# Attention with feature-major outputs: exponentials first, then the transposes of two steps back

## The reference

```python
h = rms_norm(x, g_attn) * (1.0 + scale_a) + shift_a
proj = h @ w_in                       # q_a k_a v_a c_q c_kv k_r
q_a, k_a = rope(rms_norm(q_a)), rope(rms_norm(k_a))
o_a = block_attention(q_a, k_a, v_a)  # group A: 8 query heads, 2 key heads, 64 wide
q_b = rms_norm(c_q, g_cq) @ w_uq      # group B: 8 heads, 64 plain + 32 rotary
kv  = rms_norm(c_kv, g_ckv) @ w_ukv   # keys and values of group B; k_r is shared
o_b = block_attention(q_full, k_full, v_b)
o = concatenate([rms_norm(o_a, g_out_a), rms_norm(o_b, g_out_b)]) @ w_o
x = x + gate_a * o
h = rms_norm(x, g_ffn) * (1.0 + scale_f) + shift_f
u = depthwise_conv_centred(h @ w_up, conv_w, conv_b)
x = x + gate_f * ((silu(gate) * val) @ w_down)
```

## Time and profile before

| | us |
|---|---|
| median of three runs | 1194.02 |
| the profiled execution, whole | 1194.76 |
| its span, first to last instruction | 1193.0 |
| PE busy | 1165.8 (98%) |
| DVE busy | 728.9 (61%) |
| POOL busy | 568.4 (48%) |
| ACT busy | 534.5 (45%) |

### The profile page before, as it was taken

One profiled execution on the slowest core, in us unless ns is written; L12 is line 12 of the kernel. 1 busy time (PEld: TensorE's weight loads), 2 busy tenths in 40 slices (PEclk: granted clock), 3 DMA queues, 4 the chain that ended last, 5 costly groups with the idle time before them and its releaser, 6 DMA issues.

```text
span 1193.0 us, 18770 instructions
## 1 busy us (share of the span) xinstructions
PE 1165.8 (98%) x6288; PEld 997.4 (84%) x6288; DVE 728.9 (61%) x1481; ACT 534.5 (45%) x866; POOL 568.4 (48%) x768
## 2 busy tenths in 40 slices
PE   9999999999999999999999999999999999999997
PEld 6897887998888888888789979889888888888886
DVE  5878986767766677757666438746775134412345
ACT  5347675254431344234354677635543234422432
POOL 2487500655655445644665540054555544454462
PEclk9999997999999999999999999999999999999998
DMA  9743333423445444544433202222343322332322
GB/s 350 307 168 116 92 103 107 141 72 132 174 139 207 133 166 176 194 141 176 141 110 119 75 1 89 89 89 71 124 141 106 106 86 90 106 106 74 102 89 71
DMA packets 43979, 151.55 MB, mean 127 GB/s; under 512 B 5122, under 2 KB 7810, under 8 KB 43908
## 3 DMA queue, kind: packets, MB, share of 16 engines
q1 hardware_dynamic: 43908, 150.64, 36.6%
HBM read 148.52 MB, written 2.10 MB: 126 GB/s over the span
## 4 chain that ended last, share of the span: by engine, by line
PE 46%; issue 24%; POOL 15%; POOLq 6%; DVE 6%; DVEq 2%; ACT 1%; ACTq 0%
POOL w_lo L535 14%; PE ps L614 14%; PE ps L620 14%; PE ps L615 14%; POOLq L536 5%; DVE ada_prod L1387 2%; DVEq L1389 1%; DVE nmx L1758 1%; PE ps L749 1%; PE ps L950 1%; PE ps L738 1%; PE ps L718 0%; DVE ada_prod L1608 0%; DVE o_sb L1771 0%; PE ps L726 0%
## 5 line engine op out<-in xcount | busy, mean ns | idle before, releaser
L535 POOL TENSOR_TENSOR w_lo<-w_raw,w_hi 128x256 fp32r<-128x256 f32 x712 | 532.1, 779 | 599.3 <-ACT w_hi L1117 575.7
L614 PE MATMUL ps<-h_hi,w_hi 128*128 128x512 f32 (+1 forms) x960 | 349.7, 364 | 4.2 <-DVEq L1561 2.2
L615 PE MATMUL ps<-h_lo,w_hi 128*128 128x512 f32 (+1 forms) x960 | 347.3, 362 | 0.0
L620 PE MATMUL ps<-h_hi,w_lo 128*128 128x512 f32 (+1 forms) x960 | 347.2, 362 | 0.0
L1117 ACT CAST w_hi<-w_raw 128x1024 fp32r<-128x1024 f32 x178 | 183.2, 1047 | 183.8 <-PE ps L614 183.6
L614 PEld LDWEIGHTS ps<-h_hi,w_hi 128*128 128x128 f32 x960 | 181.7, 189 | 36.8 <-DVEq L1561 3.8
L1809 DVE SCALAR_TENSOR_TENSOR u_sb<-ps,par,u_sb 128x510 f32<-128x510 f32 x176 | 131.7, 748 | 123.2 <-ACT u_sb L1345 110.2
L620 PEld LDWEIGHTS ps<-h_hi,w_lo 128*128 128x128 f32 x960 | 181.7, 189 | 27.5
L615 PEld LDWEIGHTS ps<-h_lo,w_hi 128*128 128x128 f32 x960 | 181.8, 189 | 27.2
L614 PE MATMUL ps<-a_hi,w_hi 128*128 128x512 f32 (+1 forms) x400 | 146.6, 366 | 3.3 <-DVEq L1595 2.4
L620 PE MATMUL ps<-a_hi,w_lo 128*128 128x512 f32 (+1 forms) x400 | 145.6, 364 | 0.0
(11 more groups left out here) (160 smaller groups left out, 1372.6 us busy)
## 6 DMA issues: line engine op xcount, KB each, us to landing
w_raw<-w_slots SPq DMA_DIRECT2D x178, 512.0 KB, 3.5
ada_raw<-ada_slots SPq DMA_DIRECT2D x88, 512.0 KB, 3.8
shift<-shift_slots SPq DMA_DIRECT2D x8, 512.0 KB, 13.2
x_tok<-x_rows SPq DMA_DIRECT2D x4, 512.0 KB, 9.6
x<-x_t SPq DMA_DIRECT2D x4, 512.0 KB, 13.7
y_t<-x SPq DMA_DIRECT2D x3, 512.0 KB, 2.9
y_t<-x SPq DMA_DIRECT2D x1, 256.0 KB, 3.0
y_t<-x SPq DMA_DIRECT2D x2, 128.0 KB, 2.7
```

Source lines behind the costliest of these rows:

```text
L535: nc.gpsimd.tensor_tensor(w_lo[:, j, c], w_raw[:, j, c], w_hi[:, j, c].bitcast(F32), ALU.subtract)
L614: hh = mm(out, stat[0], mov[0], start=first, stop=False)
L615: hl = mm(out, stat[0], mov[1], start=False, stop=False)
L620: return mm(out, stat[1], mov[0], start=False, stop=last)
```

## The change

- Outputs are made with features on partitions: the values are the stationary operand (64 columns for each of two heads, side by side in the array), the transposed probabilities move, 256 columns. No column of ones: ScalarE's exponentials sum their rows as they go (`accum_out`), and the probabilities are scaled before they are transposed, two of the four row blocks by VectorE, two by GpSimd (`scale_rows`).
- The transposes of the outputs and those of group B's queries go. Group B's queries are computed with features on partitions; the weights for their rotary part carry a second, swapped copy of the columns, and VectorE multiplies with a table of cosines and sines (`q_table`, one load more). Group B's scores are made of two products, plain and rotary.
- The sum of squares over features for the output norms is GpSimd's (`add_squares`) and a product of TensorE with ones (`group_sums`); ScalarE takes roots and VectorE reciprocals over the whole of 512 or 256 columns in PSUM.
- Fills, keys and one of the values are copied by VectorE instead of ScalarE, the outputs too.
- The pipeline is one step deeper. TensorE does in iteration i fill(i+1), scores(i), prob_transposes(i-2), outputs(i-3). ScalarE makes the exponentials of i first, behind a wait for the transposes of i-2, and then copies those transposes.
- The first four tiles of the output projection are each made in two parts: all first parts (group A), then all second parts.

The diff, cut to its core:

```diff
...
+    def scale_rows(j):
+        pool.wait_ge(rin_ready, NP * L + j + 1)
+        for c in (2, 3):
+            nc.gpsimd.tensor_scalar(prob[:, j % 2, c, :], prob[:, j % 2, c, :], rinv[:, j, c:c + 1], None,
+                                    ALU.mult)
+        nc.gpsimd.drain()
+        pool.sem_inc(second_scaled, 1)
+    def add_squares(j):
+        group, s, _ = PAIRS[j]
+        k, c = pair_tile(j), slice(s * SEQ, (s + 1) * SEQ)
+        total = (ssum if group == "a" else ssq_b)[:, c]
+        pool.wait_ge(o_done, NP * L + j + 1)
+        if k % 4 == 0:
+            nc.gpsimd.tensor_tensor(total, o_t[:, k, c], o_t[:, k, c], ALU.mult)
+        else:
+            nc.gpsimd.tensor_tensor(o_sq[:, 0, :], o_t[:, k, c], o_t[:, k, c], ALU.mult)
+            nc.gpsimd.drain()
+            nc.gpsimd.tensor_tensor(total, total, o_sq[:, 0, :], ALU.add)
+        nc.gpsimd.drain()
+        pool.sem_inc(o_summed, 1)
+    for i in range(NP + 1):
+        if i < NP:
+            scale_rows(i)
+        if i >= 2:
+            add_squares(i - 2)
+        if 2 <= i < 14:
+            n = L * SLOTS + S_WO + 1 + (i - 2) // 4
+            lo_quarter(n % RING, n, (i - 2) % 4)
+    lo_slots(L * SLOTS + S_WO + 4, L * SLOTS + SLOTS)
...
+def out_part(L, m, ks, release=0):
     j = slot(L, S_WO + m)
     if 0 in ks:
         wait_free(pe, L, ("wo", m))
+        pe.wait_ge(exp_ready, 4 * (NP * (L + 1) - int(m < 2)))
     for k in ks:
+        last_event = k if k < KD // 2 else k + KD // 2
+        pe.wait_ge(ot_ready, N_EVENTS * L + last_event + 1)
+        last = product(ps[:, bank(("wo", m)), :], [r[:, j, k * P:k * P + P] for r in (w_hi, w_lo)],
+                       out_operand(k, slice(0, T)), k == 0, k == KD - 1, release * int(k == ks[0]))
     if KD - 1 in ks:
+        last.then_inc(full[bank(("wo", m))], 1)
...
         pe.wait_ge(pt_ready, NP * L + j)
         for u in range(2):
+            if u == 1:
+                pe.wait_ge(second_scaled, NP * L + j + 1)
             for q in range(2):
+                if u == 0:
+                    pe.wait_ge(first_scaled, 2 * (NP * L + j) + q + 1)
...
+        for k in range(2):
+            for u in range(2):
+                v = va[:, 2 * s + k, u, :] if group == "a" else vb[:, 2 * s + k, heads[u], :]
+                last = mm(ps[64 * u:64 * u + 64, O_BANK, 0:SEQ], v, prob_t[:, j % 2, u, k, :],
+                          start=(k == 0), stop=(k == 1))
         last.then_inc(o_full, 1)
...
+    def group_sums(n):
+        pe.wait_ge(o_summed, (NP - 1) * L + (NA, NA + 4, NP - 1)[n])
+        if n == 0:
+            pe.wait_ge(qt_ready, NA * (L + 1))
+            total = ssum[:]
+        else:
+            pe.wait_ge(on_ready, N_EVENTS * L + KD // 2)
+            total = ssq_b[:, (n - 1) * SEQ:n * SEQ]
+        last = mm(sum_view(n), ones[:], total, start=True, stop=n < 2)
+        if n == 2:
+            pe.wait_ge(last_sq, L + 1)
+            last = mm(sum_view(n), ones[:], o_sq[:, 1, :], start=False, stop=True)
+        last.then_inc(group_sum, 1)
+    expand_values(0)
+    fill(0)
+    expand_values(1)
+    for i in range(NP + 3):
+        if i + 1 < NA:
             fill(i + 1)
+        if i < NP:
             scores(i)
         if i == 0:
+            expand_values(2)
+            expand_values(3)
+            expand_keys(0)
+        if i == 1:
+            expand_keys(1)
+            expand_keys(2)
+        if i == 2:
+            expand_keys(3)
+        if i == NP + 1:
+            out_part(L, 0, (0, 1))
         if 0 <= i - 2 < NP:
+            prob_transposes(i - 2)
+        if 0 <= i - 3:
+            outputs(i - 3) if i < NP + 2 else None
+        if i == NA + 3:
+            group_sums(0)
+        if i == NP - 1:
+            group_sums(1)
+    out_part(L, 0, (2, 3))
+    outputs(NP - 1)
+    out_part(L, 1, range(KD // 2))
+    group_sums(2)
     for m in range(2, TAIL):
+        out_part(L, m, range(KD // 2))
+    for m in range(TAIL):
+        out_part(L, m, range(KD // 2, KD), int(m > 0))
...
+def group_roots(L, n):
+    act.wait_ge(group_sum, 3 * L + n + 1)
+    A(sum_view(n), sum_view(n), ACT.Sqrt, bias=eps[:], scale=1.0 / 512).then_inc(group_root, 1)
+def output_hi(L, e):
+    k, c, hi, _ = event(e)
+    act.wait_ge(on_ready, N_EVENTS * L + e + 1)
+    nc.scalar.copy(hi, o_t[:, k, c]).then_inc(on_hi_ready, 1)
...
+    def take_transposes(j):
+        act.wait_ge(pt_full, NP * L + j + 1)
+        if j >= 2:
+            act.wait_ge(o_full, NP * L + j - 1)
+        nc.scalar.copy(prob_t[:, j % 2, :, :, :],
+                       ps[:, PT_BANK:PT_BANK + 2, :].rearrange("p u (k q) -> p u k q", k=2)
+                       ).then_inc(pt_ready, 1)
+    take_values(0)
+    take_values(1)
+    for i in range(NP + 2):
         if i == 0:
+            take_values(2)
+        if i >= 2:
+            act.wait_ge(pt_full, NP * L + i - 1)
+        if i < NP:
             act.wait_ge(max_ready, NP * L + i + 1)
             for c in range(4):
                 A(prob[:, i % 2, c, :], ps[:, S_BANK[i % 2] + c // 2, (c % 2) * SEQ:(c % 2 + 1) * SEQ],
+                  ACT.Exp, bias=nmx[:, i, c:c + 1], accum_out=rsum[:, i, c:c + 1]).then_inc(exp_ready, 1)
+        if i >= 2:
+            take_transposes(i - 2)
+        if i == 4:
+            split_hi(L, S_WO + 2)
+        if i == 8:
+            split_hi(L, S_WO + 3)
+        if i == NA + 4:
+            group_roots(L, 0)
+        if NA + 5 <= i < NA + 9:
+            output_hi(L, i - NA - 5)
+        if i == NP:
+            prepare(ACT.Sqrt)
+            group_roots(L, 1)
+    for e in range(KD // 2, KD):
+        output_hi(L, e)
+    group_roots(L, 2)
+    for e in range(KD, N_EVENTS):
+        output_hi(L, e)
...
+def group_inverse(L, n):
+    dve.wait_ge(group_root, 3 * L + n + 1)
+    V.reciprocal(sum_view(n), sum_view(n))
     V.drain()
+def output_scaled(L, e):
+    k, c, _, _ = event(e)
+    V.scalar_tensor_tensor(out=o_t[:, k, c], in0=o_t[:, k, c], scalar=par[:, L, PC_GOUT + k:PC_GOUT + k + 1],
+                           in1=sum_view(e // (KD // 2)), op0=ALU.mult, op1=ALU.mult).then_inc(on_ready, 1)
+def output_lo(L, e):
+    k, c, hi, lo = event(e)
+    dve.wait_ge(on_hi_ready, N_EVENTS * L + e + 1)
+    V.tensor_tensor(lo, o_t[:, k, c], hi.bitcast(F32), ALU.subtract).then_inc(ot_ready, 1)
...
+    for p in range(HEADS // 2):
+        key = ("uq", HEADS // 2 + p)
+        wait_full(dve, L, key)
+        V.tensor_tensor(halves(qr[:, p, :]), halves(ps[:, bank(key), :]),
+                        tq[:].rearrange("p (o t) -> p o t", o=1).broadcast_to([P, NSEQ, SEQ]), ALU.mult)
+        V.drain()
+        dve.sem_inc(free[bank(key)], 1)
     ada_at(L, ("in", 2))
+    def take_fill(j):
+        dve.wait_ge(qt_full, NA * L + j + 1)
+        if j >= 2:
+            dve.wait_ge(s_full, NP * L + j - 1)
+        V.tensor_copy(q_t[:, j % 2, :], ps[:, QT_BANK, 0:SEQ])
+        V.drain()
+        dve.sem_inc(qt_ready, 1)
...
+    def scale_rows(j):
+        dve.wait_ge(exp_ready, 4 * (NP * L + j + 1))
+        V.reciprocal(rinv[:, j, :], rsum[:, j, :])
+        V.drain()
+        dve.sem_inc(rin_ready, 1)
+        for c in range(2):
+            V.tensor_scalar(prob[:, j % 2, c, :], prob[:, j % 2, c, :], rinv[:, j, c:c + 1], None,
+                            ALU.mult).then_inc(first_scaled, 1)
+    def take_outputs(j):
+        _, s, _ = PAIRS[j]
+        k, c = pair_tile(j), slice(s * SEQ, (s + 1) * SEQ)
+        o = ps[:, O_BANK, 0:SEQ]
+        dve.wait_ge(o_full, NP * L + j + 1)
+        V.tensor_copy(o_t[:, k, c], o)
+        V.drain()
+        dve.sem_inc(o_done, 1)
...
+    take_fill(0)
+    for i in range(NP + 1):
+        if i + 1 < NA:
+            take_fill(i + 1)
         if i < NP:
+            maxima(i)
+        if i == 0:
+            take_values(3)
+            take_keys(0)
+        if i == 1:
+            take_keys(1)
+        if i >= 1:
+            scale_rows(i - 1)
+        if i == 1:
+            take_keys(2)
+        if i == 2:
+            take_keys(3)
+        if i < NP:
             ada_step(L, i, 0)
+        if i >= 3:
+            take_outputs(i - 3)
         if i < NP:
             ada_step(L, i, 1)
+        if i == NA + 5:
+            group_inverse(L, 0)
+            output_scaled(L, 0)
+            output_scaled(L, 1)
+        if i == NA + 6:
+            output_lo(L, 0)
+            output_scaled(L, 2)
+        if i == NA + 7:
+            output_lo(L, 1)
+            output_scaled(L, 3)
+        if i == NP:
+            output_lo(L, 2)
+            output_lo(L, 3)
+    take_outputs(NP - 2)
+    group_inverse(L, 1)
+    for e in range(KD // 2, KD):
+        output_scaled(L, e)
+    take_outputs(NP - 1)
+    for e in range(KD // 2, KD):
+        output_lo(L, e)
+    group_inverse(L, 2)
+    for e in range(KD, N_EVENTS):
+        output_scaled(L, e)
+    for e in range(KD, N_EVENTS):
+        output_lo(L, e)
```

More of the change, by code:

```diff
@@ L106, with pair_tile @@
 NP = len(PAIRS)
-VW = HD + 1
+NA = NP // 2
+def pair_tile(j):
```

(42 more changed lines are left out.)

418 lines of the change are left out of this document (138 added, 280 removed).

## The result

The changed kernel takes 1240.66 us (median of 4 runs, 1239.37 to 1242.52) against 1193.44 for the kernel before (4 runs, 1190.72 to 1194.55): a ratio of 1.040, 95% interval 1.0378 to 1.0423. The forecast was 1228 with a range of 1204 to 1248: slower, the side that was forecast, and 12.7 us beyond the number. The profiled execution has a span of 1240.7 us where it was 1193.0, so 47.7 us are to be found.

The account below looks back on a forecast made before the run. It took VectorE to pace the steps with adaLN, TensorE's step being hardly longer in layer 1. 1194.02 + 25.0 (layer 1) + 6.0 (layer 2) + 3 (behind the projection) = 1228 us, range 1204 to 1248.

Parts of the forecast that it names:

- Start of layer 1: Before layer 1's attention: first maximum at 113.6, +8.5 us, as VectorE waits for the last query products before its adaLN.
- Steps of layer 1: Layer 1's 16 attention steps: 108.0 us against 82.5, +25.5, with port, copies and group A's norm included.
- The port: Attention steps: VectorE and GpSimd wait for each other's instructions, 0.8 us a step taken, bounds 0 and 1.5.
- the halves stay at 1.22 beside a busy GpSimd: Steps with adaLN: a sign that the forecast is wrong; it expected adaLN halves of more than 1.22 us.
- The reciprocal of 512 columns: Group A's norm, once a layer on VectorE: 3.1 us, bounds 0.5 to 3.1.
- rival (4): Attention steps: the new order doesn't decouple engines, late GpSimd work holds quick steps; +13 us; chance 0.08 with worse.
- rival (2): Attention steps: TensorE, busy some 60% of a step, gets the lower clock for stretches; about +13 us, 1241; chance 0.20.
- Tail of layer 1: From the steps' end to the output projection's last full tile: 26.8 us against 35.8, -9.0.
- Behind the projection: After the output projection: late slot release and four x updates within 11 us beside adaLN, +3 us for both layers.
- Layer 2: Second layer's attention: start +2.7, steps +7.5 (eight without adaLN at 3.9 us each), tail -4.2; together +6.0 us.
- Rival (1): Attention steps: the port costs nothing, half of GpSimd's work can lie behind PSUM reads; -17 us, 1211; chance 0.18.
- Rival (3): Attention steps: TensorE paces and its savings pass through if VectorE's adaLN step stays under about 4.9; 1188; chance 0.09.

Follow-up runs that it names:

- e4: Group B's first-sequence sum stands on TensorE behind step 14's transposes and step 13's outputs, against the changed kernel: 1235.32 us.
- the kernel with everything together: Changed kernel plus ScalarE copying outputs and group A's fills, tail sum and two adaLN products moved, GpSimd scaling rows by TENSOR_TENSOR: 1224.90 us.

## Why the prediction was right in sign and 13 us short

By its own steps, in the profiled execution:

- **Start of layer 1**: +8.5 forecast, +7.8 measured, by the mechanism named; the run with the adaLN products moved shows that 5 of it was their place.
- **Steps of layer 1**: +25.5 forecast, +22.7 measured (20.6 between the maxima, and a last step of 6.8 instead of 4.7). The list of VectorE's instructions was right: 5.1 forecast in group B without collisions, 5.22 measured. The port was half as dear as taken, 0.41, and fell on other instructions. The prediction named as a sign against it that the halves stay at 1.22 beside a busy GpSimd, and in the repeated step they do: the price is on the pair of row scalings, 1.09 instead of 0.61. The reciprocal of 512 columns took 3.37 (forecast 3.1), and shortening it gave 2.9 a layer. The step of 6.87 wasn't forecast: GpSimd had fallen behind, TensorE waited 2.2 us for it and then made its scores at the lower clock. That is rival (4) with a piece of rival (2), for single steps; with short scalings on GpSimd it is 5.63.
- **Tail of layer 1**: -9.0 forecast. From the last step's end at 218.2 to TensorE's end of the second halves at 249.2 it is 31.0 where it was 35.8, so -4.8. The term that failed is the 26.8 us for the new tail: it left out a wait that the change adds. The sum over group B's first sequence goes into the PSUM bank of group A's, may start only when VectorE's last scaling has read that, and stands on TensorE ahead of the transposes of step 14. With the sum moved the tail is 27.5.
- **Behind the projection**: +3 for both layers forecast, with the reason right (x is updated four times within 11 us beside adaLN) and the size wrong. From TensorE's end (223.5, now 249.2) to ScalarE's first copy of the feed-forward part it was 43.5 us and is 49.7, +6.2 in layer 1 alone; with short adaLN halves it is 43.7. Before and after:

```profile
267.04 1.43 ACT L1345 ACTIVATE u_sb<-ps,par 128x512 f32<-128x512 f32 x2
```

```profile
298.93 1.43 ACT L1374 ACTIVATE u_sb<-ps,par 128x512 f32<-128x512 f32 x2
```

- **Feed-forward of layer 1**: nothing forecast, +0.2 measured.
- **Layer 2**: start +2.7 forecast, +2.6 measured. Steps +7.5 forecast, +12.0 measured (9.9 and a last step of 6.8). The quick ones took 4.2 instead of 3.9. The 3.9 came from GpSimd's list, and GpSimd doesn't hold them: emptied, it leaves them at 29.1. The ring of 4.01 us through TensorE and ScalarE does, which "ScalarE is close by", 3.3 us, left out. It is the first half of rival (4), that the new order doesn't decouple the engines. The odd 5.81 adds the lower clock: outputs of 1.98 us where they take 1.08, and 4.28 in e4, whose granted clock was 1.00 there. The steps with adaLN hold two of the 6.87 kind (6.91 and 7.35, TensorE waiting 1.84 and 2.22 us for GpSimd's scaling). Here the GpSimd row scaling is the mis-sized term, 0.98 us without a collision (1.96 a pair) and 1.3 on average, not 0.45. The nearest row of the kernel before, with half the columns and a constant factor, already took 0.53:

```profile
L553 POOL TENSOR_SCALAR gqk<-gqk 128x128 f32<-128x128 f32 x1 | 0.5, 533 | 0.3 <-issue 0.3
```

The tail and the rest of layer 2: -2.7 forecast, +1.1 measured: the same wait at the sum, 5.98 us there.

The misses add up: -0.7 - 2.8 + 4.2 + 4.7 + 0.2 - 0.1 + 4.5 + 3.8 = 13.8, against 47.7 - 34.0 = 13.7 (1.5 of the 3 is counted in each layer). Two of the errors worked against each other: with the measured 0.41 for the port's 0.8 in 24 steps, the sum would have been 9 us lower, 1219. So the port's price, twice too high, covered part of what was left out, and a miss of only 13 us is in part luck. The measured time is that of rival (2), 1241, but not by its mechanism: at the full clock the repeated steps kept their length. Rival (1) was tried by emptying GpSimd: 9.3 us, not 17. Rival (3) fell with VectorE's back-to-back steps of 5.63, above the 4.9 from which it would decide; that TensorE's step became 4.0, as forecast (3.9), was seen once VectorE was relieved.

The Trainium skill (GPSIMD Engine Reference, Specifications) says that GpSimd contends with those VectorE instructions that have two SBUF inputs or run in a two-port mode. The runs agree for the adaLN halves: GpSimd's scalings waited for them (3.95 us a pair against 1.96). VectorE's row scaling reads one SBUF tensor, and no run here shows whether it works in a two-port mode. Measured, it is delayed too, and by how much hangs on what GpSimd runs: its TENSOR_SCALAR beside it costs 0.15 us a pair (0.76 against 0.61), its TENSOR_TENSOR 0.76 (1.37).

Left open: why the kernel with ScalarE's output copies spreads over 7 us between executions, what the five added matmuls cost in the tail one by one, and why the kernel with everything together is still 30 us above the kernel before.
